# Fox-attention and mixture-of-experts trunk on one core: another order of projection pairs, four more gate tiles projected as seven-product pairs instead of inside attention, and 128 columns in the last key tile's product

## The reference

```python
z = x @ w_in                                  # 1024 x 4104
q, k, v, f, glu_a, glu_g, sc_b, sc_c, sc_h = jnp.split(z, IN_SPLITS, axis=-1)
br_att = fox_attention(q, k, v, f + b_forget)       # 8 heads of 64, causal
u = causal_depthwise_conv(glu_a * sigmoid(glu_g), conv_w) + conv_b   # 31 taps
br_conv = silu(layer_norm(u, ...))
br_sc = sc_b * causal_depthwise_conv(sc_c * sc_h, sc_w)              # 3 taps
for n, br in enumerate((br_att, br_conv, br_sc)):
    gate = sigmoid(x @ w_gate[n] + b_gate[n])       # 1024 x 1024 each
    merged += gate * (br @ w_branch[n])
h = merged @ w_out
```

## Time and profile before

| | us |
|---|---|
| median of three runs | 1612.54 |
| profiled execution, whole | 1612.83 |
| its span, first to last instruction | 1611.2 |
| TensorE busy in the span | 1537.8 (95%) |
| DVE, ACT, POOL busy | 1248.8, 899.3, 457.3 |
| chain that ended last: TensorE / DMA / DVE | 79% / 7% / 5% |

### The profile page before, as it was taken

One profiled execution on the slowest core, in us unless ns is written; L12 is line 12 of the kernel. 1 busy time (PEld: TensorE's weight loads), 2 busy tenths in 40 slices (PEclk: granted clock), 3 DMA queues, 4 the chain that ended last, 5 costly groups with the idle time before them and its releaser, 6 DMA issues.

```text
span 1611.2 us, 20596 instructions
## 1 busy us (share of the span) xinstructions
PE 1537.8 (95%) x7507; PEld 1275.9 (79%) x7507; DVE 1248.8 (78%) x1551; ACT 899.3 (56%) x1263; POOL 457.3 (28%) x405
## 2 busy tenths in 40 slices
PE   7999999998999999999999997999999999999980
PEld 6778888887888888888888886888888888887770
DVE  6988968679666666645855777999999999988875
ACT  5533332333556555536312335888888888887773
POOL 3977777776112212000000011111111111111210
PEclk9999999999999999999999999999999999999995
DMA  4155243574523332144734678999999999999966
GB/s 160 41 116 99 80 92 83 111 119 98 155 80 106 92 99 82 59 164 118 256 120 143 188 270 298 355 369 385 366 358 352 358 358 345 352 342 361 365 220 220
DMA packets 160671, 335.62 MB, mean 208 GB/s; under 512 B 18064, under 2 KB 87696, under 8 KB 160571
## 3 DMA queue, kind: packets, MB, share of 16 engines
q1 hardware_dynamic: 146986, 304.64, 57.6%
q0 software_dynamic: 13584, 29.67, 6.4%
HBM read 299.89 MB, written 51.66 MB: 218 GB/s over the span
## 4 chain that ended last, share of the span: by engine, by line
PE 79%; DMA 7%; DVE 5%; ACT 1%; issue 1%; POOL 0%; SPq 0%; DVEq 0%; POOLq 0%; ACTq 0%
PE ps L987 27%; PE ps L1367 25%; PE ps L1029 19%; DMA e_raw<-in_w_down 5%; PE ps L1142 2%; DVE e_lo L2379 2%; PE ps L1127 2%; DMA e_raw<-in_w_up 1%; PE ps L1374 1%; PE ps L1307 1%; DVE zout L2442 1%; PE ps L1382 1%; DVE zout L2435 1%; DMA z_d<-ye,row_i 0%; PE ps L1274 0%
## 5 line engine op out<-in xcount | busy, mean ns | idle before, releaser
L2379 DVE TENSOR_TENSOR e_lo<-e_raw,e_hi 128x1024 fp32r<-128x1024 f32 x376 | 436.1, 1220 | 26.0 <-ACT e_hi L1756 21.6
L1756 ACT ACTIVATE e_hi<-e_raw 128x1024 fp32r<-128x1024 f32 x376 | 367.8, 1050 | 25.8 <-DMA e_raw<-in_w_down 19.2
L1029 PE MATMUL ps<-ts,w_hi 128*128 128x512 f32 x576 | 177.3, 389 | 0.3 <-POOL w_lo L806 0.3
L1367 PE MATMUL ps<-e_hi,xe_hi 128*128 128x512 f32 x512 | 164.0, 401 | 9.1 <-DVE e_lo L2379 8.5
L1446 ACT ACTIVATE w_hi<-w_raw 128x512 fp32r<-128x512 f32 x127 | 79.8, 630 | 155.3 <-PE ps L1029 80.0
L1367 PE MATMUL ps<-e_lo,xe_hi 128*128 128x512 f32 x512 | 159.3, 393 | 0.0
L1367 PE MATMUL ps<-e_hi,xe_lo 128*128 128x512 f32 x512 | 158.5, 391 | 0.0
L1937 DVE SCALAR_TENSOR_TENSOR ps<-upad,cols,ps 128x1024 f32<-128x1024 f32 x116 | 148.9, 1283 | 4.3 <-ACT ps L1470 2.7
L987 PE MATMUL ps<-xt_hi,w_hi 128*128 128x512 f32 x320 | 126.5, 405 | 8.0 <-DVE w_lo L1877 6.3
L1029 PEld LDWEIGHTS ps<-ts,w_hi 128*128 128x128 f32 x576 | 108.1, 188 | 23.0 <-issue 0.7
L987 PE MATMUL ps<-xt_hi,w_lo 128*128 128x512 f32 x320 | 122.5, 392 | 0.0
(11 more groups left out here) (354 smaller groups left out, 3354.1 us busy)
## 6 DMA issues: line engine op xcount, KB each, us to landing
e_raw<-in_w_up SPq DMA_DIRECT2D x128, 1024.0 KB, 21.6
e_raw<-in_w_down SPq DMA_DIRECT2D x64, 1024.0 KB, 21.9
w_raw<-in_w_in SPq DMA_DIRECT2D x56, 256.0 KB, 4.5
w_raw<-in_w_gate SPq DMA_DIRECT2D x47, 256.0 KB, 3.5
gate_s<-gates_d SPq DMA_DIRECT2D x22, 512.0 KB, 3.6
gates_d<-gate_t POOLq DMA_DIRECT2D x16, 512.0 KB, 3.5
qkv_d<-qs SPq DMA_DIRECT2D x12, 512.0 KB, 5.7
w_raw<-in_w_branch SPq DMA_DIRECT2D x24, 256.0 KB, 4.7
```

The costliest lines, as they stand in the source:

```text
L1029: last = nc.tensor.matmul(ps[:, bank, :], w[:, c % RING, k, :], mv, start=k == 0 and n == 0, stop=k == KC - 1 and n == PASSES - 1)
L1367: last = nc.tensor.matmul(ps[:, banks + h, :], st[:, s, :], w[:, s0 % RSPL, h * HALF:(h + 1) * HALF], start=s == 0 and m == 0, stop=s == n ...
L1756: nc.scalar.activation(e_hi[:, (UPT + s) % RSPL, :], e_raw[r][:, s % 2, :], ACT.Copy).then_inc(e_h, 1)
L2379: nc.vector.tensor_tensor(e_lo[:, sp_, :], e_raw[raw_slot(b, s)][:, s % 2, :], e_hi[:, sp_, :], ALU.subtract).then_inc(e_all, 1)
```

## The change

`PAIRS` has 20 entries. The rounds 0 to 2 are (h, c), (b, q), (a, g), (k, v), round 2 with one (m, n) before (k, v); the last round is (h, c), (m, n), (b, q), (m, n), (m, n), (m, n), (k, v). There are five (m, n) pairs in the place of three, so ten gate tiles instead of six come from pairs. `GT`, the gate tiles computed in attention, goes from 16 to 12: `gate_step(n)` gives a gate quarter to three of every four steps, and none to the steps 3 and 7 of each head. The order of pairs lets the taps start earlier; all 124 fit beside the pairs up to pair 16. POOL, not DVE, makes the low parts of the first two gate blocks of attention. `scores(0)` waits for the last `add` of the last pair (c21), not for the one before it. `attend` multiplies only the 128 valid columns of the last key tile, and `clear_p` with its semaphore is gone. Where pairs of gates follow each other, `stored` makes the adds wait for the pair before to be stored.

```diff
-    PAIRS += [("h", "c", _r), ("b", "q", _r)] + ([("m", "n", _r), ("a", "g", _r + 1)] if _r + 1 < CT else []) + [("k", "v", _r)]
+    PAIRS += [("h", "c", _r)] + ([("b", "q", _r), ("a", "g", _r + 1)] if _r + 1 < CT else [("m", "n", 1), ("b", "q", _r), ("m", "n", 2), ("m", "n", 3), ("m", "n", 4)])
+    PAIRS += ([("m", "n", 0)] if _r == 2 else []) + [("k", "v", _r)]
-GT = 2 * KT
+GATES = 2 * KT
+GT = GATES - 4
-            return FIRST <= c < CB and (c - FIRST) % UNITS not in LO_DVE
+            return FIRST <= c < CB + 2
+        def gate_step(n):
+            return n // 4 * 3 + n % 4 if n < STEPS and n % 4 < 3 else None
+        def stored(s, kind):
+            users = [p for p in range(s) if (PAIRS[p][0] in "mk" if kind in "mk" else PAIRS[p][1] in "nqv")]
+            last = [p for p in range(s) if PAIRS[p][0] in "bmk"]
+            if not users:
+                return 0
+            return 16 * STORES[last[-1] if last[-1] < s - 1 else users[-1]]
@@ POOL
             split_qk(0)
+            pool.wait_ge(qk_l, 2)
+            split_w(CB)
+            split_w(CB + 1)
-            (clear_p, its waits and its calls)
-                    pool.wait_ge(p_zero, 6 + 4 * (n // TT))
+                    pool.wait_ge(qk_l, 2 * (n // TT + 1))
@@ TensorE
                 elif n == 0:
-                    pe.wait_ge(c_add, added(NP - 1, "c12"))
+                    pe.wait_ge(c_add, added(NP - 1, "c21"))
-                for k in range(nk):
+                order = [(0, 0, 0), (nk - 1, 0, P), (nk - 1, 1, P), (0, 1, 0)] + [(k, i, 0) for k in range(1, nk - 1) for i in range(2)]
+                for k, i, c0 in order:
-                        last = nc.tensor.matmul(o_bank(j), v, p[n % 2][:, k, :], start=k == 0 and s == 0, stop=k == nk - 1 and s == 1)
+                    last = nc.tensor.matmul(o_bank(j)[:, c0:2 * P], v, (pt_hi, pt_lo)[i][n % 2][:, k, c0:2 * P], ...)
-                gate_half(n)
+                if gate_step(n) is not None:
+                    gate_half(gate_step(n))
@@ DVE, after the last pair
             while done < CT * CTAPS:
                 tap(done, conv_link)
                 done += 1
-            split_w(CB)
-            split_w(CB + 1)
```

More of the change, by code:

```diff
@@ L103 @@
 HERE = 2
-QKV_STORES = 3 * CT + KT - HERE
+QKV_STORES = 3 * CT + KT - HERE + GATES - GT
 STREAM = [("g", _i, _h) for _i in range(HERE) for _h in range(2)] + [("b", _t, 0) for _t in range(NBR * KT)]
@@ L122 @@
                 _n += 1
-CONV_STORE = {5: 0, 9: 1, 14: 2}
+CONV_DONE, _n = [], 0
+for _s in range(NP):
+    for _j in range(UNITS):
+        _room = CTAPS * (1 + sum(_s > _p + (_j < 2) for _p in TILE_PAIR.values()))
+        for _ in range(TAPS[_s][_j]):
+            if _n < min(_room, CT * CTAPS):
+                _n += 1
+                if _n % CTAPS == 0:
+                    CONV_DONE.append(_s)
+CONV_STORE = {_s + 1: _i for _i, _s in enumerate(CONV_DONE[:CT - 1])}
+FIRST_LOAD = max(TILE_PAIR[CT - 1] + 2, CONV_DONE[CT - 2] + 1)
+STORES = [sum(dict(b=1, m=2, k=2).get(_p[0], 0) for _p in PAIRS[:_s + 1]) for _s in range(NP)]
 BANKS = (0, 1, 2, 3, 6, 7)
@@ L315, in program @@
         qkv_d = nc.dram_tensor("qkv_d", [3, W, SEQ], FP32, kind="Internal").ap()
-        gates_d = nc.dram_tensor("gates_d", [GT + KT, P, SEQ], FP32, kind="Internal").ap()
+        gates_d = nc.dram_tensor("gates_d", [GATES + KT, P, SEQ], FP32, kind="Internal").ap()
         conv_d = nc.dram_tensor("conv_d", [W, SEQ], FP32, kind="Internal").ap()
@@ L445, in wait_lo @@
             else:
-                e.wait_ge(lo_ok, sum(not by_pool(i) for i in range(min(c + 1, CB))) + max(c + 1 - CB, 0))
+                e.wait_ge(lo_ok, sum(not by_pool(i) for i in range(c + 1)))
         def whole(c):
@@ L459, in raw_loads, with gate_of @@
             return 1 if c < FIRST else 1 + NP + (c - CB) // RING + 1
[L461 to L466, removed]
+        def gate_of(i, n):
+            return HERE + 2 * i + n if HERE + 2 * i < KT else KT + GT + 2 * i + n - (KT - HERE)
+        def gate_step(n):
[6 more added lines that the diff above has]
+            return 16 * STORES[last[-1] if last[-1] < s - 1 else users[-1]]
         def wait_x(e, t):
@@ L513, in block @@
                     if kind in "mn":
-                        w, col = w_gate[0, 0], (HERE + 2 * i + "mn".index(kind)) * P
+                        w, col = w_gate[0, gate_of(i, "mn".index(kind)) // KT], gate_of(i, "mn".index(kind)) % KT * P
                     else:
@@ L553, in store_pair @@
                     for n in range(2):
-                        sp.dma_start(gates_d[GT + HERE + 2 * i + n], qs[1 - n][:]).then_inc(qkv_out, 16)
+                        sp.dma_start(gates_d[(gate_of(i, n) - KT) % (GATES + KT)], qs[1 - n][:]).then_inc(qkv_out, 16)
                 elif one == "k":
@@ L616, in _ @@
                     store_conv(CONV_STORE[s])
-                if s == TILE_PAIR[CT - 1] + 2:
+                if s == FIRST_LOAD:
                     load_qk(0)
@@ L627, in _ @@
             for n in range(STEPS):
-                m, q = n // 4, n % 4
+                g = gate_step(n)
                 if n % TT == 6 and n // TT + 2 < HEADS:
@@ L632, in _ @@
                     load_v(n // (2 * TT) + 1)
-                if q < 2:
-                    raw(CB + 2 * (m + 2) + q)
+                if g is not None and g % 4 < 2:
+                    raw(CB + 2 * (g // 4 + 2) + g % 4)
             def load_wo(k):
@@ L849, in _ @@
             split_qk(0)
+            pool.wait_ge(qk_l, 2)
+            split_w(CB)
+            split_w(CB + 1)
             pool.wait_ge(w_used, RING + chunk(NP - 1, 4) + 1)
             load_aug(1)
[L853 to L866, removed]
-            for n in range(STEPS):
[L869 to L876, removed]
+            for n in range(STEPS):
                 if n % TT == 0 and 2 <= n // TT + 1 < HEADS:
                     load_aug(n // TT + 1)
-                if n % 4 == 1 and n >= 4:
-                    store_gate(n // 4 - 1)
+                g = gate_step(n)
+                if g is not None and g % 4 == 1 and g >= 4:
+                    store_gate(g // 4 - 1)
                 if n % TT == 3 and n // TT + 1 < HEADS:
-                    pool.wait_ge(p_zero, 6 + 4 * (n // TT))
+                    pool.wait_ge(qk_l, 2 * (n // TT + 1))
                     split_qk(n // TT + 1)
@@ L1138, in attend @@
                     pe.wait_ge(v_l, 2 * (n // (2 * TT)) + 2)
-                for k in range(nk):
+                order = [(0, 0, 0), (nk - 1, 0, P), (nk - 1, 1, P), (0, 1, 0)] + [(k, i, 0) for k in range(1, nk - 1) for i in range(2)]
+                for k, i, c0 in order:
                     v = v_two[:, k, 2 * u:2 * u + 2, :].rearrange("p b d -> p (b d)")
-                    for s, p in enumerate((pt_hi, pt_lo)):
-                        last = nc.tensor.matmul(o_bank(j), v, p[n % 2][:, k, :], start=k == 0 and s == 0, stop=k == nk - 1 and s == 1)
+                    last = nc.tensor.matmul(o_bank(j)[:, c0:2 * P], v, (pt_hi, pt_lo)[i][n % 2][:, k, c0:2 * P],
+                                            start=(k, i) == (0, 0), stop=(k, i, c0) == order[-1])
                 last.then_inc(o_ok, 1)
@@ L1487, in second @@
                     for n in range(2):
-                        b = ROW_BGATE * CT + HERE + 2 * PAIRS[s][2] + n
+                        b = ROW_BGATE * CT + gate_of(PAIRS[s][2], n)
                         last = nc.scalar.activation(dest(s, n), dest(s, n), ACT.Tanh, scale=0.5,
@@ L1607, in _ @@
             for n in range(STEPS + 2):
-                i, g, m, q = n // (2 * TT), n % (2 * TT), n // 4, n % 4
+                i, g, w = n // (2 * TT), n % (2 * TT), gate_step(n)
                 if n >= 2:
@@ L1616, in _ @@
                     split_v(i, 1 if g == 1 else 0)
[L1617 to L1622, removed]
+                if w is not None and w % 4 == 2:
+                    gate_tanh(w // 4, 0)
+                if w is not None and w % 4 == 0 and w >= 4:
+                    gate_tanh(w // 4 - 1, 1)
+                if n == STEPS:
+                    gate_tanh(GT - 1, 1)
+                if w is not None and w % 4 < 2:
+                    split_w(CB + 2 * (w // 4 + 1) + w % 4)
                 if 1 <= n % TT <= 3 and n // TT + 1 < HEADS:
@@ L1912, in add @@
                 elif kind and kind in "qkvmn":
-                    dve.wait_ge(qkv_out, stored(kind, i))
+                    dve.wait_ge(qkv_out, stored(s, kind))
                 nc.vector.tensor_tensor(dst, ps[:, bank_of(s, j), :], held, ALU.add).then_inc(c_add, 1)
@@ L2067, in _ @@
                     split_v(i, 1 if g == 1 else 0)
-                if n < STEPS and q < 2:
-                    split_w(CB + 2 * (m + 1) + q)
+                if w is not None and w % 4 < 2:
+                    split_w(CB + 2 * (w // 4 + 1) + w % 4)
             def split_wo(k):
```

6 lines of the change are left out of this document (2 added, 4 removed).

## The result

The changed kernel takes 1624.1 us (median of five runs, 1620.61 to 1628.78) against 1613.87 us of the kernel before (five runs beside them, 1611.35 to 1615.19): a ratio of 1.0064, 95% interval 1.005 to 1.0078. It is slower, by 10.2 us, twice the 5.0 us forecast, and 2.1 us above the upper end of the range. The profiled execution took 1624.1 us, its span is 1622.4.

What follows compares the result with a forecast made beforehand. TensorE's own instructions were taken to bound projection and attention. 38.1 + 0.5 - 5.4 - 26.0 - 2.2 = +5.0 us gave 1617.5 us, range 1614 to 1621 (1609 to 1622 including some rivals).

Steps and rivals of the forecast that it cites:

- Two pairs: Projection: four gate tiles come back as two pairs of 84 matmuls at 0.2269 us, +38.1 us of TensorE time.
- projection* rival: Projection: adds waiting for stores, or crowded taps, cost 1 to 1.5 us at four seams; 1622 us, chance 0.09.
- Start of attention: End of projection to the first matmul of gate quarter 4: 18.3 us in place of 23.7, -5.4 us.
- Steps 3 and 7 and the end: Attention: removed gate quarters save only part of their 2.85 us each, the rest becoming waits; -26.0 us together.
- faster* rival: Attention: TensorE never waits in the thin steps, so 45.6 us are saved there; 1598 us, chance 0.13 in full or mostly.
- port* rival: Step 3, even heads: normalize gets the port before POOL's subtraction, some 1.4 us back in four heads; 1612 us, chance 0.09.
- the clock: Attention: the clock falls behind the new 2.4 to 2.5 us waits, +1.5 to +6 us; 1619 to 1624 us, chance 0.11.
- a granted clock below 1 inside attention: Sign in the profile after that was listed as showing the forecast wrong.
- The early wait of pair 2: Projection: TensorE's early 1.90 us wait for a weight block could change by -1.9 to +1.9 us; taken as +0.5.
- The rest of the kernel: Merge, output projection and experts: claimed untouched, difference 0.
- The narrow products: Attends: 64 matmuls cut from 256 to 128 columns, 0.085 us each instead of 0.119; -2.2 us, between 0 and -3.8.
- step 3 of the odd heads: Attention: next transposes wait for `split_pt` behind an added weight rounding; 1.76 us saved in each of four heads, -7.1 us.

Runs made afterwards that it cites:

- the third experiment: Changed kernel with the eight small forget-row stores issued behind the last two weight loads of pair 2 instead of ahead of them: 1620.45 us, ratio 1.0045.
- the second experiment: Changed kernel with POOL's two subtractions in step 3 held until DVE's normalize of that step has ended: 1615.19 us, ratio 1.0006.
- the first and sixth: Changed kernel each time: missing gate quarters moved to steps 1 and 5, 1609.23 us; 12 unused 512-column products in each step without a quarter, 1646.79 us.
- the last four experiments: Changed kernel, waits filled: 1620.84 us; changed kernel, quarters as unused work: 1646.79; kernel before, narrow products only: 1612.88; changed kernel, quarters and stores moved, POOL held: 1606.85.
- both edits: Changed kernel with missing quarters moved to steps 1 and 5 and forget stores issued behind pair 2's weight loads: 1607.82 us, ratio 0.9963.
- the narrow product alone: Kernel before with only the last key tile's products cut to 128 columns and POOL's zero fills removed: 1612.88 us, ratio 0.9995.

## Why the prediction was right or wrong

**Right: the mechanism and the sign.** A change that takes 24 products of 512 columns away on balance (5.4 us at 0.2269) makes the kernel slower, since the steps it thins out had to cover DVE, ACT and POOL. By its own terms:

- Two pairs, +38.1. 1512 products in 344.62 us include one fall of the clock; 1512 x 0.2269 are 343.1. No new wait for stores, taps or POOL. The *projection* rival did not happen.
- Start of attention, -5.4. From the end of the projection (435.30) to the gate quarter of step 4 (453.06) it takes 17.8 us, forecast 18.3. c21 costs 0.9 instead of 1.1. ACT's q rounding starts 9.2 us after the end of the projection, 0.5 sooner than assumed (9.7).
- Steps 3 and 7 and the end, -26.0. In a profile without falls in attention (the third experiment) attention is 272.6 us; the prediction says 306.3 - 33.6 = 272.7 (how far this is luck stands below). Two heads take 64.83 us in the profile after, where the forecast of 32.3 a head gives 64.6. POOL's hold on normalize is shown by the second experiment, the role of the cover by the first and sixth.
- The *faster* rival is refuted for steps 3 and 7. The *port* rival did not come by itself, as forecast; forced by a wait it gave 4.7 us of the 5.6 named, and 3.1 more since the falls of the clock were gone too.

**Wrong: the size.** The sum was 5.0 us, measured 10.2 (11.2 between the spans). Of the 6.2 us between 5.0 and 11.2, attention has 3.0, the projection 1.1 and the rest of the kernel 2.1.

1. The step that failed is the clock. The prediction priced it as a rival, at 0.11, and at zero in the sum, arguing that a wait of 2.68 us had left the clock alone and that mine were shorter. In the profile after, the clock fell behind waits of 3.00, 2.58 and 2.20 us. Each fall cost about 1.5 us, 4.6 in all. The measured 1624.1 lies at the upper end of that rival's 1619 to 1624. The prediction named "a granted clock below 1 inside attention" as the sign of this, and it was there. One row of a wait without a fall was no bound: the wait of the earlier trace rows is 2.60 to 2.86 us long in nine of the ten profiles, and in four of them (the last four experiments) a fall goes with it. The price of a likely but not certain fall belonged into the sum.
2. The early wait of pair 2 was taken at +0.5 us and grew by 1.1 (1.90 to 3.00). The prediction's bound of +1.9 held it. It added little to the miss, since in this profile the first pair starts 0.7 us sooner than before (49.34 for 50.04 us; over all profiles 48.7 to 50.2), which is variation and so luck. But the fall behind the wait was not seen as a possibility in the projection at all.
3. The rest of the kernel is 2.1 us longer in this profile, forecast 0. The last stretch at half clock but one, near 1577 us, is 6.8 us long there and 3.4 before; the 24 products at it take 8.66 us in place of 7.36, which is 1.3 of it. Over the profiles of all kernels here this part varies from 908.1 to 912.4 us, and it goes with the clock: the four profiles that have 6.8 us at half clock in it ahead of the kernel's end take 908.1 to 909.5, the six that have 10.2 to 20.5 us take 911.3 to 912.4. So I count it as variation of the clock. That the change has no part in it was not shown: both profiles of the old projection are among the four.

This division of the miss holds for the profiled execution, which is the median of the five. Of the other four only the mean granted clock is on record, 0.982 to 0.985 beside the profiled 0.984; where in them the clock fell is not known.

The narrow products are a term mis-sized the other way: -2.2 forecast, -0.6 measured. The pace of 0.085 us was read from two products with nothing but a mask product behind them; in an attend the weight loads, 0.11 us apart, set the pace. The 1.6 us were made up by a start of attention 0.5 us shorter than forecast and by step 3 of the odd heads, which saved 2.07 in place of 1.76, 1.2 us in four heads. So the agreement of the stage within 0.1 us is luck; the single steps agree within 0.3.

## What to carry to other kernels

When filler work is taken out of a pipelined loop, its worth depends on the step it leaves: walk through each step by what its successors wait for, and take it from the steps that have most work of their own. Here the whole change cost 10 us with the quarters missing in one place and gained 5 with them missing in another. Where TensorE is left with a wait of the length behind which the clock fell here (1.76 to 3.60 us), add the price of a half-clock stretch times a chance to the sum, and take the chance from several profiles.

## What the hardware showed beyond what was expected

- The clock falls behind waits of like length in one profile and not in another: behind 2.58 us in the changed kernel but not in the third experiment, behind 2.20 us in one of three heads, behind 1.76 us with both edits but not behind the 1.75 and 1.76 us of two other profiles, behind 1.90 us with the narrow product alone but not in the kernel before. Behind the wait of 3.60 us in the expert stage it fell in all ten profiles. Ahead of the kernel's end every fall lasted 3.4 us or double, at a granted clock of one half. Whether filling a wait with unused products keeps the clock up stays open.
- What POOL's subtraction holds up moves with the order of the two engines. With POOL held back, normalize went from 1.48 to 0.35 us in step 3 of even heads and from 0.62 to 1.49 in step 4. In an odd head the next normalize started first, at 551.32, and kept its 0.62 us; now POOL's second subtraction took 2.73 us in place of 2.40, and DVE's low part of a weight block behind it 2.88 in place of 0.69 (second experiment, timelines of POOL and DVE):

```profile
551.46 2.73 POOL L835 TENSOR_TENSOR q_low<-q_raw,q_dup 64x1024 fp32r<-64x1024 f32 x1
...
551.32 0.62 DVE L2037 TENSOR_SCALAR prob<-prob,rinv 128x768 f32<-128x768 f32 x1
551.86 2.88 DVE L1883 TENSOR_TENSOR w_lo<-w_raw,w_hi 128x512 fp32r<-128x512 f32 x1
```

The Trainium skill, "SBUF — State Buffer", section "Who interferes with whom", tells of a lock on shared ports that whoever issues first holds for the whole instruction. These rows agree: with the order of issue reversed, the hold-up fell on the other engine.

- Halving the columns of 64 products from 256 to 128 saved 0.6 us of a nominal 3.8.
